# Softmax of chunked attention: dividing the exponentials by their row sums pair by pair, ahead of the transposes, in place of scaling the head outputs

## What is computed

```python
def one_chunk(c):
    s = jnp.einsum('bihd,bjhd->bhij', q_c, k_c).astype(jnp.float32) + bias
    valid = (c * CHUNK - pad + band_pos) >= 0
    p = jax.nn.softmax(jnp.where(valid, s, NEG_INF), axis=-1)
    return jnp.einsum('bhij,bjhd->bihd', p.astype(v_c.dtype), v_c)
...
h = layer_norm(DEEPNORM_ALPHA * h + y, ln_g[i, 0], ln_b[i, 0])
```

## Time and profile before

| what | value |
|---|---|
| three runs | 1219.03, 1220.73, 1221.91 us (median 1220.73) |
| the profiled execution | 1221.01 us, of which its span is 1219.2 us |
| PE busy | 1192.9 us, 98% of the span |
| POOL busy | 529.4 us, 43% |
| ACT busy | 422.5 us, 35% |
| DVE busy | 373.3 us, 31% |
| PE's share of the chain that ended last | 91% |
| attention of layer 1 | about 654 to 808 us of the span |

### The profile page before, as it was taken

One profiled execution on the slowest core, in us unless ns is written; L12 is line 12 of the kernel. 1 busy time (PEld: TensorE's weight loads), 2 busy tenths in 40 slices (PEclk: granted clock), 3 DMA queues, 4 the chain that ended last, 5 costly groups with the idle time before them and its releaser, 6 DMA issues.

```text
span 1219.2 us, 14860 instructions
## 1 busy us (share of the span) xinstructions
PE 1192.9 (98%) x5690; PEld 987.9 (81%) x5690; DVE 373.3 (31%) x599; ACT 422.5 (35%) x666; POOL 529.4 (43%) x286
## 2 busy tenths in 40 slices
PE   8999989999999999999999999999999999999997
PEld 6878868988888888888887777787988888888886
DVE  4050162732222221000603555536322222220005
ACT  4353234332322322113325666652332322322211
POOL 4529416144444444447155334463344444444441
PEclk9999999999999999999999999999999999999999
DMA  6433213162222222224031212132222222222221
GB/s 210 146 124 127 104 35 107 39 224 81 102 103 103 94 79 103 104 104 164 26 104 70 87 45 86 49 134 70 105 99 78 99 103 103 101 75 100 104 69 69
DMA packets 22109, 119.76 MB, mean 98 GB/s; under 512 B 2464, under 2 KB 6944, under 8 KB 9136
## 3 DMA queue, kind: packets, MB, share of 16 engines
q1 hardware_dynamic: 16304, 107.06, 24.9%
q10 hardware_dynamic: 5760, 12.07, 3.0%
HBM read 117.02 MB, written 5.24 MB: 100 GB/s over the span
## 4 chain that ended last, share of the span: by engine, by line
PE 91%; DVE 3%; ACT 2%; POOL 2%; DMA 1%; issue 1%; SPq 0%; DVEq 0%; POOLq 0%; ACTq 0%
PE bank L1226 28%; PE bank L1228 28%; PE bank L1227 28%; PE bank L1553 2%; PE bank L1541 2%; PE bank L1288 1%; PE bank L1575 1%; PE bank L1574 1%; DMA s_x_t<-x_t 1%; POOL s_w_lo L791 1%; DVE s_g_c L1030 1%; POOL s_early L791 0%; DMA s_raw<-stream 0%; DVE s_bn_o L1109 0%; ACT s_g_on L610 0%
## 5 line engine op out<-in xcount | busy, mean ns | idle before, releaser
L791 POOL TENSOR_TENSOR s_w_lo<-s_raw,s_w_hi 128x1024 fp32r<-128x1024 f32 x183 | 440.0, 2408 | 528.3 <-ACT s_w_hi L456 528.3
L456 ACT ACTIVATE s_w_hi<-s_raw 128x1024 fp32r<-128x1024 f32 x183 | 192.3, 1058 | 403.2 <-PE bank L1228 383.0
L1226 PE MATMUL bank<-s_t_hi,s_w_hi 128*128 128x512 f32 x832 | 326.3, 392 | 0.0
L1228 PE MATMUL bank<-s_t_hi,s_w_lo 128*128 128x512 f32 x832 | 324.1, 389 | 0.0
L1227 PE MATMUL bank<-s_t_lo,s_w_hi 128*128 128x512 f32 x832 | 323.8, 389 | 0.0
L1228 PEld LDWEIGHTS bank<-s_t_hi,s_w_lo 128*128 128x128 f32 x832 | 156.2, 188 | 33.2
L1226 PEld LDWEIGHTS bank<-s_t_hi,s_w_hi 128*128 128x128 f32 x832 | 156.2, 188 | 31.6
L1227 PEld LDWEIGHTS bank<-s_t_lo,s_w_hi 128*128 128x128 f32 x832 | 156.3, 188 | 31.3
L1226 PE MATMUL bank<-s_w_hi,s_a_hi 128*128 128x512 f32 x352 | 137.1, 390 | 0.0
L1228 PE MATMUL bank<-s_w_hi,s_a_lo 128*128 128x512 f32 x352 | 137.0, 389 | 0.0
L1227 PE MATMUL bank<-s_w_lo,s_a_hi 128*128 128x512 f32 x352 | 136.9, 389 | 0.0
(11 more groups left out here) (155 smaller groups left out, 1171.1 us busy)
## 6 DMA issues: line engine op xcount, KB each, us to landing
s_raw<-stream SPq DMA_DIRECT2D x97, 1024.0 KB, 4.8
s_ln_gb<-ln_gb ACTq DMA_DIRECT2D x4, 1024.0 KB, 4.8
bias_rows<-rel_bias ACTq DMA_DIRECT2D x1, 3072.0 KB, 14.0
s_h<-x ACTq DMA_DIRECT2D x1, 2048.0 KB, 12.9
s_r_b<-bias_rows ACTq DMA_DIRECT2D x16, 128.0 KB, 2.5
s_x_t<-x_t SPq DMA_DIRECT2D x3, 512.0 KB, 11.4
out<-s_h SPq DMA_DIRECT2D x3, 512.0 KB, 2.6
s_raw<-stream SPq DMA_DIRECT2D x2, 256.0 KB, 3.8
```

What stands on the lines that cost most here:

```text
L456: nc.scalar.activation(w_parts(n, slice(0, SLAB))[0], raw[:, pair % RAWS, n % 2, :], ACT.Copy).then_inc(hi_done, 2 if n == 1 else 1)
L791: nc.gpsimd.tensor_tensor(lo, raw[:, place // 2 % RAWS, n % 2, :], hi.bitcast(F32), ALU.subtract).then_inc(lo_done, 2 if n == 1 else 1)
L1226: nc.tensor.matmul(out, l_hi, r_hi, start=start, stop=False, skip_group_check=skip)
L1228: return nc.tensor.matmul(out, l_lo, r_hi, start=False, stop=stop, skip_group_check=skip)
```

## The change

The exponentials are now divided as soon as they exist. Behind the other work of a step DVE runs `divide(step)`: it waits for both exponentials of the step, takes the reciprocals of their two row sums (128x2), waits for that result, and multiplies the two tiles of `r_p` in place, each by its own column of `inv_sum`. PE's `turn_weights` waits for the multiplication (`p_scaled`) where it waited for the exponential. `invert_sums`, `spread_inverse`, `turn_inverse` and `scale_heads` are gone, with the buffer `inv_wide` and the waits on them; `pair_high` waits for `head_sum`.

```diff
@@ -243,7 +243,6 @@
         r_b = get("r_b", [P, 2, 2, SEQ])
         r_o += [get(f"r_o{p}", [P, SEQ]) for p in range(RPA_PAIRS // 2, RPA_PAIRS)]
         r_half = get("r_half", [P, SEQ])
-        inv_wide = get("inv_wide", [P, PAIR_UNITS, RPA_D])
 
         get, _ = carve(gb_at, region)
         r_p = get("r_p", [P, 4, SEQ])
@@ -338,9 +337,7 @@
         exp_done = sem("exp_done")
         v_lo_done = sem("v_lo_done")
         inverted = sem("inverted")
-        inv_spread = sem("inv_spread")
-        inv_turned = sem("inv_turned")
-        o_scaled = sem("o_scaled")
+        p_scaled = sem("p_scaled")
         p_turned = sem("p_turned")
         p_hi = sem("p_hi")
         p_lo = sem("p_lo")
@@ -700,7 +697,7 @@
             def pair_high(p):
                 if p == 0:
                     act.wait_ge(slab_done, RPA_OUT)
-                act.wait_ge(o_scaled, p + 1)
+                act.wait_ge(o_summed, 2 * p + 2)
                 nc.scalar.activation(t_hi[:, p, :], r_o[p][:, :], ACT.Copy).then_inc(o_hi, 1)
 
             def exponents(s):
@@ -710,15 +707,6 @@
                     act.wait_ge(p_turned, s - 3)
                 nc.scalar.activation(r_p[:, s % 4, 0:(t + 1) * P], bank[2 + hd][:, 0:(t + 1) * P], ACT.Exp,
                                      bias=neg_max[:, s:s + 1], scale=-1.0, accum_out=row_sum[:, s:s + 1]).then_inc(exp_done, 1)
-
-            def spread_inverse(p):
-
-                act.wait_ge(inverted, p + 1)
-                if p >= 1:
-                    act.wait_ge(inv_turned, p)
-                units = inv_sum[:, p * PAIR_UNITS:(p + 1) * PAIR_UNITS]
-                nc.scalar.activation(inv_wide[:, :, :], units.unsqueeze(2).to_broadcast([P, PAIR_UNITS, RPA_D]), ACT.Copy
-                                     ).then_inc(inv_spread, 1)
 
             FIRST_HIGH = UNITS // 2 - TILES - 1
             act.wait_ge(normed[1], TILES)
@@ -738,10 +726,8 @@
                 if t != 1:
                     exponents(2 * step)
                     exponents(2 * step + 1)
-                if p >= 1 and t == 0:
-                    spread_inverse(p - 1)
-                    if ahead:
-                        load_bias(p + 1)
+                if p >= 1 and t == 0 and ahead:
+                    load_bias(p + 1)
                 if p >= 1 and t == 1:
                     head_half(2 * p - 2)
                     head_half(2 * p - 1)
@@ -757,7 +743,6 @@
             weights_high(UNITS - 1)
             act.wait_ge(p_turned, UNITS)
             load_gb(2)
-            spread_inverse(RPA_PAIRS - 1)
             head_half(RPA_HEADS - 2)
             head_half(RPA_HEADS - 1)
             pair_high(RPA_PAIRS - 2)
@@ -1148,10 +1133,16 @@
                 nc.vector.tensor_tensor_reduce(out=blk, in0=blk, in1=r_b[:, p % 2, hd, SEQ - keys:], scale=1.0, scalar=-NEG_INF,
                                                op0=ALU.add, op1=ALU.min, accum_out=neg_max[:, s:s + 1]).then_inc(s_biased, 1)
 
-            def invert_sums(p):
-                units = slice(p * PAIR_UNITS, (p + 1) * PAIR_UNITS)
-                dve.wait_ge(exp_done, (p + 1) * PAIR_UNITS)
-                nc.vector.reciprocal(inv_sum[:, units], row_sum[:, units]).then_inc(inverted, 1)
+            def divide(step):
+
+                both = slice(2 * step, 2 * step + 2)
+                dve.wait_ge(exp_done, 2 * step + 2)
+                nc.vector.reciprocal(inv_sum[:, both], row_sum[:, both]).then_inc(inverted, 1)
+                dve.wait_ge(inverted, step + 1)
+                for s in (2 * step, 2 * step + 1):
+                    keys = (unit(s)[1] + 1) * P
+                    nc.vector.tensor_scalar(r_p[:, s % 4, 0:keys], r_p[:, s % 4, 0:keys], inv_sum[:, s:s + 1], None,
+                                            ALU.mult).then_inc(p_scaled, 1)
 
             def weights_low(s):
                 _, t, hd = unit(s)
@@ -1166,12 +1157,6 @@
                 dve.wait_ge(o_half, hd + 1)
                 nc.vector.tensor_tensor(r_o[hd // 2][rows, :], bank[6 + hd % 2][rows, :], r_half[rows, :],
                                         ALU.add).then_inc(o_summed, 1)
-
-            def scale_heads(p):
-
-                dve.wait_ge(o_summed, 2 * p + 2)
-                dve.wait_ge(inv_turned, p + 1)
-                nc.vector.tensor_tensor(r_o[p][:, :], r_o[p][:, :], bank[6][:, :], ALU.mult).then_inc(o_scaled, 1)
 
             def last_pair_low():
 
@@ -1193,8 +1178,6 @@
                 p, t = step // TILES, step % TILES
                 bias_and_max(2 * step)
                 bias_and_max(2 * step + 1)
-                if p >= 1 and t == 0:
-                    invert_sums(p - 1)
                 if step >= 1:
                     weights_low(2 * step - 2)
                     weights_low(2 * step - 1)
@@ -1205,14 +1188,11 @@
                 if p >= 1 and t == 2:
                     head_sum(2 * p - 2)
                     head_sum(2 * p - 1)
-                if p >= 1 and t == 3:
-                    scale_heads(p - 1)
-            invert_sums(RPA_PAIRS - 1)
+                divide(step)
             weights_low(UNITS - 2)
             weights_low(UNITS - 1)
             head_sum(RPA_HEADS - 2)
             head_sum(RPA_HEADS - 1)
-            scale_heads(RPA_PAIRS - 1)
             last_pair_low()
             layer_norm(2, FFN_IN[1])
             feed_forward(1, FFN_IN[1])
@@ -1545,7 +1525,7 @@
 
             def turn_weights(s):
                 _, t, hd = unit(s)
-                pe.wait_ge(exp_done, s + 1)
+                pe.wait_ge(p_scaled, s + 1)
                 if s >= 2:
                     pe.wait_ge(p_lo, s - 1)
                 for j in range(t + 1):
@@ -1553,21 +1533,11 @@
                     last = nc.tensor.transpose(bank[4 + hd][:, at * P:(at + 1) * P], r_p[:, s % 4, j * P:(j + 1) * P], ident[:, :])
                 last.then_inc(p_turned, 1)
 
-            def turn_inverse(p):
-
-                pe.wait_ge(inv_spread, p + 1)
-                pe.wait_ge(o_summed, 2 * p + 1)
-                for t in range(TILES):
-                    last = nc.tensor.transpose(bank[6][:, t * P:(t + 1) * P],
-                                               inv_wide[:, 2 * t:2 * t + 2, :].rearrange("p u d -> p (u d)"), ident[:, :])
-                last.then_inc(inv_turned, 1)
-
             def weights_v(hd):
 
                 pe.wait_ge(p_lo, PAIR_UNITS * (hd // 2) + PAIR_UNITS - 1 + hd % 2)
                 if hd >= 2:
                     pe.wait_ge(o_summed, hd - 1)
-                    pe.wait_ge(o_scaled, hd // 2)
                 for j in range(TILES):
                     out, blocks = bank[6 + hd % 2][:, j * P:SEQ], key_blocks(hd % 2, j)
                     v_parts = r_v[:, j, hd, :, :].rearrange("p a d -> p (a d)")
@@ -1599,8 +1569,6 @@
                 if step >= 1:
                     turn_weights(2 * step - 2)
                     turn_weights(2 * step - 1)
-                if p >= 1 and t == 3:
-                    turn_inverse(p - 1)
                 if p >= 1 and t == 1:
                     weights_v(2 * p - 2)
                     weights_v(2 * p - 1)
@@ -1626,14 +1594,11 @@
                     pe.wait_ge(p_lo, UNITS)
                 if t == 3:
                     pe.wait_ge(o_summed, RPA_HEADS)
-                    pe.wait_ge(o_scaled, RPA_PAIRS)
 
             def rpa_beside(_, k):
                 if k == 1:
                     weights_v(RPA_HEADS - 2)
                     weights_v(RPA_HEADS - 1)
-                if k == 2:
-                    turn_inverse(RPA_PAIRS - 1)
             out_projection(RPA_OUT, KD, t_hi, t_lo, 2, rpa_out_ready, rpa_out_free, [(0, 1), (2, 3)], rpa_beside, early=True)
             feed_forward(1, FFN_IN[1], 2)
             ffn_out(1, 3)
```

## The result

| | before | after |
|---|---|---|
| median, us (7 runs each) | 1219.77 (1218.42 to 1221.91) | 1224.99 (1221.31 to 1226.26) |
| ratio, 95% interval | | 1.0039 [1.0024, 1.0055] |
| profiled execution, span, us | 1221.01, 1219.2 | 1226.14, 1224.4 |

The account below looks back on a forecast made before the run. PE, busy 98% of the span, was taken as the bound. Waits and lower clock less removed transposes, 3.3 + 1.7 + 1.1 + 4.2 - 2.2 = 8.1 us, on 1221.01 gave 1229.1 us; own range 1226.5 to 1231.5, wide range 1221.0 to 1233.0.

Parts of the forecast that it names:

- all three places: Pair 0 t = 1, pair 7 t = 1, and pair 7 t = 2 and 3, where POOL was to hold the multiplications.
- the case with the chance of 0.62: The forecast itself: POOL holds the multiplications at the ends; 8.1 us slower, 1229.1 us, chance 0.62.
- not-held case: Rival: the multiplications don't wait for POOL, only DVE's own lateness costs; +0.6 us, 1221.6 us, chance 0.22.
- (a) wait of pair 0: Pair 0, t = 1: POOL's subtraction starts first and holds the multiplications; PE waits 3.3 us.
- (a) lower clock behind it: After PE's stop in pair 0, the granted clock drops to its lower level for most of two windows; 1.7 us.
- (b) pair 7, t = 1: POOL's subtraction and then its next turn delay the two multiplications; PE waits 1.1 us.
- (c) pair 7, t = 2 and 3: POOL takes a turn between t = 2's multiplications (3.0 us), delaying the last units' bias and exponentials; 4.2 us together.
- removed groups, pairs 1 to 5: Transposes gone from t = 3 of these pairs, where PE is full: 5 x 0.44 = 2.2 us saved.
- the lower clock once more in pair 7: Counted only in the upper bound, with the longest multiplications: 10.5 us slower, 1231.5 us.
- Multiplication: DVE's new multiplication of an SBUF tile: 0.59 us at 512 columns, 0.47 at 384, 0.36 at 256, 0.25 at 128.
- POOL in between in each t = 3: Rival: POOL holds each t = 3's second multiplication, 2.4 us in each of pairs 0 to 5; about 1243 us, chance 0.11.
- Everything fits: Rival: multiplications not held and short as a memset, pair 7 loses less; at best 1219.5 us, chance 0.05.

Follow-up runs that it names:

- e2_accum: Changed kernel with the multiplications given an added zero and an accumulated output into an unused column; ratio 0.9991 to the kernel before.
- the gates: Changed kernel with POOL made to wait for the multiplications: in pair 0 alone, ratio 1.0012 to the kernel before; in pairs 0 and 7, 0.9988.
- e1_again: The changed kernel, unedited, timed once more; ratio 1.0045 to the kernel before.
- e5_before: The kernel before, unedited, run once more; ratio 0.9999 to the kernel before.
- e8_before_third: The kernel before, unedited, profiled a third time; one execution, no ratio, first scores at 652.3 us.
- e10_tiny: Kernel before with six 128x1 memsets of an unused tile added on VectorE, t = 0 of pairs 1 to 6; ratio 1.0003 to the kernel before.
- e11_sems: Kernel before with two unused semaphores declared, no instruction added or removed; ratio 1.0000 to the kernel before.
- e7_hybrid: Pairs 1 to 6 divide ahead as in the changed kernel, pairs 0 and 7 normalise as in the kernel before; ratio 0.9975 to the kernel before.
- e4_no_division: Kernel before without reciprocals, spread, turned spread and scaling of head outputs, output not normalised; ratio 0.9968 to the kernel before.
- e9_hybrid_swap: Pairs 1 to 6 divide ahead, pairs 0 and 7 as before, with pair 1's t = 3 multiplications ahead of scale_heads(0); ratio 0.9973 to the kernel before.

## Why the prediction was right, and where it was wrong

**The direction and the mechanism held.** The choice on which it rested, that the multiplication belongs with the operations that POOL holds, is confirmed in all three places by the timeline, and by e2_accum and the gates as causes. The kernel is slower, as the case with the chance of 0.62 had it.

**The size did not.** 1224.99 us lies below the forecast's own range, 1226.5 to 1231.5. It is in the wide range only because that was drawn down to 1221.0 for the sake of the not-held case, which the runs refute. That part of the hit is luck. In differences, 5.2 us were measured where 8.1 were forecast.

**The terms.** In differences of PE's milestones against the profile before:

| term | predicted | measured |
|---|---|---|
| (a) wait of pair 0 | 3.3 | 3.0 |
| (a) lower clock behind it | 1.7 | 2.9 here, 1.7 in e1_again |
| (b) pair 7, t = 1 | 1.1 | 0.8 |
| (c) pair 7, t = 2 and 3 | 4.2 | 3.8 |
| removed groups, pairs 1 to 5 | -2.2 | -2.15 |
| sum, attention | 8.1 | 8.3 here, 7.1 in e1_again |

The sum of (c) hides two errors that nearly cancel. Its t = 2 wait was 2.27 us (0.40 and 1.87), not 3.0; and behind it came 1.7 us of lower clock, which the prediction had only in its upper bound ("the lower clock once more in pair 7").

**Multiplication.** I took 0.59 us at 512 columns, the middle of two bounds. It took 0.48 where it had to wait for nothing (0.35 at 256, where two took 0.62, and 0.28 at 128). The estimate from the Trainium skill (VectorE: DVE Perf Modes, The perf-mode tier table), 0.43, was the nearer one. The rows agree with double rate for this operation: from 128 to 512 columns it grows by 0.20 us, the accumulated form of e2_accum by 0.40 (0.34 to 0.74). It is worth little, as the prediction said.

The Trainium skill (SBUF — State Buffer, Who interferes with whom) says that such a `tensor_scalar` on the shared port is blocked for the whole of a GpSimd instruction that had the port first. The trace agrees: 2.72 us for two that take 0.62 alone.

**What failed** is the step of the sum that adds the 8.1 us to the whole profiled time of before, "The profiled execution took 1221.01 us, 0.3 above the median: 1229.1 us". It assumes that all in front of the attention stays as it was. It did not: PE's program is 32 matmuls and some waits shorter, and its first scores came 3.1 us earlier, in a stretch that no line of the diff touches. In this pair of profiles that is all of the difference between 8.3 us in the attention and 5.2 in the span. No row of before could have shown it.

A second, smaller part: the profile before was one with the short stretch at the lower clock in pair 7, which e5_before and e8_before_third show at 1.7 us more. Take the mean of the five profiles with that attention, e10_tiny and e11_sems included, against the changed kernel's two. To the last `weights_v` it is 154.6 and 161.5 us, 7.0 longer; the first scores are at 653.7 and 650.2, 3.4 earlier. That leaves 3.5, with the medians at 5.2 and 4.1 in the two comparisons; so few profiles don't fix it closer. Of the 3.4 us, 1.7 is clock lost ahead of the first scores (5.1 and 3.4 us in the means).

**The rivals.** *Not held* is refuted: the multiplications that began inside a subtraction of POOL, in pair 0 and in pair 7's t = 1, ended behind it. e2_accum is that case, made: its wait in pair 0 is 1.03 us, where the rival had 1.0; its attention is 1.9 us longer, not 0.6. The form is slower by itself, which the rival didn't have; how much of the 1.3 us that explains was not measured. *POOL in between in each t = 3* didn't come: the second multiplication starts 0.3 us before POOL, where the estimate had 0.1. e7_hybrid shows that the mechanism is real and what a pair costs, 1.75 us and not the 2.4 of the prediction. *Everything fits* is out with the first.

## What to carry to other kernels

Work moved from a full engine to an idle one must be looked at by its port, not by its engine's busy share: here the new DVE work was free in the middle, where a pair takes 19.05 us, the same as in e4_no_division without any division. Three collisions with POOL at the ends cost five times what the change saved (5.9 + 0.8 + 3.8 against 2.15). Where such an operation meets a long POOL instruction, either make sure which of the two starts first (a wait on POOL, or another order on DVE: two multiplications begun 0.13 us ahead of POOL lost 1.75 us, begun 0.73 us ahead nothing), or take a form that isn't held, even if it is slower by itself. And before a difference of a few us is laid to a change, compare when the untouched stretches begin and end: e9_hybrid_swap beats both kernels (0.9973), but with PE's program padded it doesn't measurably (0.9996), so most of that gain is probably not its softmax. Its attention is 1.8 us shorter than the mean of the five, 0.15%.

## What was unexpected of the hardware

- The same multiplication with an accumulated output (`TENSOR_SCALAR_CACHE_REDUCE`) isn't held by POOL: two of 256 columns ran within 0.89 us (659.11 to 660.00) beside the subtraction beside which the plain two took 2.72. Alone it is the slower one, 0.74 against 0.48 us at 512 columns.
- In the attention, what the lower clock cost behind a stop of PE of 1.8 to 3.0 us came in two sizes only, 1.7 and 3.4 us, and the same program had either in its profiles. Elsewhere a stop of that length often cost no clock at all: one of 2.00 us near 88 us was followed by granted clock 0.50 in six of the fourteen profiles and by full clock in eight, and in the first 20 us stops of 2.59 us (e4_no_division) and 2.39 us (e10_tiny) were followed by full clock, one of 2.36 us (e2_accum) by 0.50.
- Waits of 0.90 and 1.03 us in pair 0 were followed by no lower clock; the one of 3.00 us was, both times.
- With 48 waits at the end of PE's program SP issued two transfers of the first 8 us in 1.97 us instead of 1.13, and PE's first scores came 2.7 us later (one profile each). The count of instruction packets did not change with it.
